# The merge stage's widening products as three float32r passes, with their weights in the split ring, the merge's entry and exit waits and the row stage's pacing changed

## The chip, the cores and the metric

One Trainium2 chip; the kernel runs on one NeuronCore. The metric is the device time of one launch in microseconds (us). Its engines are TensorE (PE in the profile; PEld is its weight loads), VectorE (DVE), ScalarE (ACT), GpSimd (POOL) and SyncE (SP), which issues the DMAs. Each has its own in-order instruction stream, and they meet at semaphores.

## The reference, cut to what matters

Three blocks are applied to x, a [1024 tokens, 1024 features] float32 matrix. The change lies in the last part of the first block:

```python
branches = jnp.stack([y_a, y_b, y_c], axis=0)               # three branches, 256 wide each
up = jnp.einsum('nbtw,nwd->nbtd', branches, w_up)           # widened to 1024: the "up" products
gates = jax.nn.sigmoid(jnp.stack([gate_logits_a, gate_logits_b, gate_logits_c], axis=0))
merged = jnp.sum(gates * up, axis=0)
out = jnp.einsum('btd,de->bte', merged, w_out)
return layer_norm(DEEPNORM_ALPHA * x + out, ln_g, ln_b)
```

The second block begins with an RMS norm of this result and a projection of it (its v columns are computed in the same stage as `out`).

## The kernel before, in words

Everything is float32. Large products are made from float32r operands: a value is split into a high half (ScalarE copies it as float32r) and a low half (VectorE subtracts the high half from it), and one product becomes three passes, high x high, low x high, high x low (`mm3`, L260, the passes at L263, L264 and L265).

Weights come in **units** of [128, 1024]. `Weights` (L287) keeps a ring of two raw units and of three split ones. SP loads unit i+1 when unit i-1 has been split (`w_load`, L313), ScalarE writes its high half (`w_hi_of`, L325, instruction at L332) once PE has finished the unit three before, VectorE the low half (`w_lo_of`, L340, instruction at L345). `early_units` lists all units in the order in which they are used; `OUT_W0`, `V_W0` and others are positions in that list. Each engine's program is a Python generator. `weave` advances several of them in turn, one `STEP` at a time, so the number of `STEP`s sets the order of instructions in an engine's stream.

Before the merge, gate tiles 0 to 15 (branches a and b) are computed as units, copied out and stored in DRAM. The merge then has eight steps, one for each d, a tile of 128 output features by 1024 tokens:

- PE (`merge_pe`, L933): one gate unit for branch c (`unit_pe`, 48 float32r passes of 512 columns), then `up_pe` for each of the three branches: 2 contraction tiles x 2 token halves, each one plain fp32 matmul (L928) of a 128x128 block of w_up with yT, the branch outputs transposed. So 12 such products per step. Banks of PSUM come from a ring of eight, `B.all`.
- ScalarE (`merge_act`): splits a weight unit, applies the sigmoid to two gate tiles read back (L1198), then to the gate unit's two halves (L1179).
- VectorE (`merge_dve`): splits a weight unit, then multiplies each product with its gate (L1521) and adds it to the merged tile (L1524), branch by branch.
- SP (`step_load`): reads back two gate tiles of 512 KB and loads three blocks of w_up of 128 KB into the tile `up` and one slot of h.

Ahead of the merge PE waits until the last early gate has been evicted (`sig_u`) and until VectorE has written the last part of yT (`ye`, L1501).

After the merge comes the **row stage**, `rows1_*`: 48 units, each used as the moving operand for groups of three, three and two token tiles (`GROUPS`). Units 0 to 23 of the stage are `out` (8 per group), units 24 to 47 are v (8 per group). A unit takes 18 passes for a group of three tiles and 12 for a group of two, L263 to L265. The merged tiles, as stationary operand, are split first: `m_hi` on ScalarE (L1241), `m_lo` on VectorE (L1589), tile 0 at the end of the merge, the others one per unit. When a group's 8 `out` units are done, VectorE adds x (L1607, "orow"), then come the layer norm's statistics (L1621), its root on ScalarE (L1272) and its two passes on VectorE (L1638, L1641); then the RMS norm of `norm_act`, `norm_dve` and `norm_pe`: squares (L437), scaling (L447), eight banks of PE transposes (L496), and the split of their results into `xs` (L457 on ScalarE, L482 on VectorE). PE has two banks for these transposes, so the third bank waits for the low half of the first. These programs are woven with the 48 units, two `STEP`s per unit. They begin at `OUT_AT` = 16, 32, 48 with different offsets on each engine.

Of the kernel before, what the change touches and what calls it, by code (L numbers as in the profile page):

```python
# [286 lines left out]
class Weights:  # L287
    def __init__(self, K, stack, units, first, depth=2, width=1024):
        self.units, self.first, self.start, self.depth, self.width = units, first, first, depth, width
        self.buf = K.sb(stack, "wring", [128, depth, width])  # L290
        self.parts = K.sb(stack, "wparts", [128, PARTS, 2, width], F32R)

    def raw(self, i):
        return self.buf[:, i % self.depth, :]

    def part(self, i, x):
        return self.parts[:, i % PARTS, x, :]
# [226 lines left out]
def b1_layout(K, A, st, h, xT, xs, W):  # L524
# [8 lines left out]
    up = K.sb(st, "up", [128, 4, 256])  # L533
# [23 lines left out]
    B.up = [[up[:, 0, :], up[:, 1, :]], [up[:, 2, :], up[:, 3, :]], [slots[2][:, 0:256], slots[2][:, 256:512]]]  # L557
# [10 lines left out]
    B.units, B.mm, B.all = Ring(K, K.banks[0:3]), Ring(K, K.banks[3:8]), Ring(K, K.banks)  # L568
# [67 lines left out]
def b1_sp(K, A, B):  # L636
# [13 lines left out]
    for i in range(2, ATT_W0 + 3):  # L650
        if i == 42:
# [3 lines left out]
            nc.sync.dma_start(B.h[:, 3:8, :], A["x"][:, 3:8, :]).then_inc(*sp.done("x_again", 0, by=16))  # L655
# [50 lines left out]
def up_load(K, A, B, j):  # L706
    br, d = divmod(j, 8)
    if d >= 2:
        K.sp.wait_ge(*(yield "up", j - 2, 1))
    K.nc.sync.dma_start(B.up[br][d % 2], A["wg"][j][:, 1024:1280]).then_inc(  # L710
        *K.sp.done("up_load", j, slot=f"{br}{d % 2}", by=16))


def step_load(K, A, B, d):
# [3 lines left out]
    for j in (d, 8 + d, 16 + d):  # L718
        yield from up_load(K, A, B, j)
# [197 lines left out]
def up_pe(K, B, j):  # L917
    nc, pe, br = K.nc, K.pe, j // 8
    pe.wait_ge(*(yield [("sb_y", 31), ("ye", 1, 0, 1), ("ye", 2, 1, 1)][br]))
    pe.wait_ge(*(yield "up_load", j))  # L920
    w = columns(B.up[br][j % 2])
# [4 lines left out]
    for k in range(2):  # L926
        for h, (b, _) in enumerate(banks):
            a = nc.tensor.matmul(b, w[:, k, :], B.yT[:, 2 * br + k, half(h)], start=(k == 0), stop=(k == 1))  # L928
            if k:
                a.then_inc(*pe.done("up", j, h))  # L930


def merge_pe(K, B):  # L933

    for d in range(8):
        yield from unit_pe(K, B.W, gate_unit(EARLY + d), B.xs, B.xkeys, B.all, "sig_u")
        for br in range(3):
            yield from up_pe(K, B, 8 * br + d)
# [3 lines left out]
def b1_pe(K, A, B):  # L942
# [9 lines left out]
    pe.wait_ge(*(yield "sig_u", gate_unit(EARLY - 1), 1))  # L952
    pe.wait_ge(*(yield "ye", 2, 1, 1))
# [4 lines left out]
    yield from weave(rows1_pe(K, B), *[later(OUT_AT[g] + 12, norm_pe(K, B, 2, g, B.turn)) for g in range(3)])  # L958
# [278 lines left out]
def m_hi(K, B, i):  # L1237
    K.act.wait_ge(*(yield "u", OUT_W0 - 1, 1))
# [28 lines left out]
def norm1_act(K, B, g):  # L1267
# [5 lines left out]
    yield STEP  # L1273
    yield STEP
# [318 lines left out]
def rows1_dve(K, B):  # L1593
    nc, dve = K.nc, K.dve
    for n in range(48):
        if n < 7:
            yield from m_lo(K, B, n + 1)
        if n == 8:
            for part in range(2):
                dve.wait_ge(*(yield "x_again", part))  # L1600
        if n in (8, 16, 24):
            for t in GROUPS[n // 8 - 1]:
# [11 lines left out]
def norm1_dve(K, B, g):  # L1614
# [20 lines left out]
    for t in ts:  # L1635
# [6 lines left out]
            *dve.done("ln_b", t))  # L1642
        yield STEP
# [2154 lines left out]
def build_program(nc, A):  # L3798
    with ExitStack() as ctx:
# [106 lines left out]
def host1(I):  # L3906
# [10 lines left out]
    A["wg"]=np.ascontiguousarray(np.concatenate([G,U],2))  # L3917
# [85 lines left out]
```

## Time and profile before

| | us |
|---|---|
| median of 3 runs | 2908.21 |
| lowest, highest | 2908.03, 2910.93 |
| profiled execution | 2909.24 |
| its span, first to last instruction | 2907.9 |

The mean granted TensorE clock of the profiled execution is 0.986 of full speed. In a timeline row the first number is the start in us from the span's start, the second the duration in us; in brackets stands the idle time of the engine before it and what ended it ("issue": nothing that the profile shows). `ps` is PSUM, `wparts` the split weights, `wring` the raw ones, `xs` the split left operand, `merged`, `xT`, `h` and `b1t` tiles in SBUF. PE's matmuls are pipelined, so a pass's duration is longer than the distance between the starts of two. In a window row the length of the window comes first, then for PE, PEld, DVE, ACT and POOL the busy us with the number of instructions, then the granted clock, the DMA share and GB/s.

### The profile page before, as it was taken

What the parts mean: (1) busy time and instruction counts of PE and PEld (TensorE: products, weight loads), DVE (VectorE), ACT (ScalarE), POOL (GpSimd) and SP (SyncE); (2) the same over time, 40 slices, a digit from 0 to 9 for tenths busy, and PEclk for the clock granted to TensorE, in tenths of its full rate; (3) what the DMA queues carried; (4) which work ended last, traced back from release to release, by engine and by line L of the source; (5) the groups of instructions that cost most, each with busy time, mean ns of one, the idle gap of its engine ahead of it and who ended that gap; (6) DMA issues with size and microseconds to landing.
All of it is one profiled execution on the core that took longest, in us unless ns stands there. A gap on an engine that the chain in (4) does not pass through costs nothing.

```text
span 2907.9 us, 52327 instructions
## 1 busy us (share of the span) xinstructions
PE 2781.6 (96%) x21208; PEld 2181.1 (75%) x21208; DVE 1663.6 (57%) x3141; ACT 1268.5 (44%) x2321; POOL 222.5 (8%) x281
## 2 busy tenths in 40 slices
PE   8999999999999899999999999999898889999998
PEld 6766777776667777777777777777888878778776
DVE  3555656663347625655555556766566664652566
ACT  4344534322224536655556544344444434642234
POOL 0000000000000001111111001455310000000000
PEclk9999999999999999999999999999999999999999
DMA  3010120124224561343332334355844364521114
GB/s 129 30 37 30 44 58 30 52 73 166 89 80 129 159 191 46 82 104 81 85 83 74 111 112 154 131 167 186 287 134 162 126 247 139 160 91 44 37 61 156
DMA packets 188368, 316.58 MB, mean 109 GB/s; under 512 B 78288, under 2 KB 119520, under 8 KB 186464
## 3 DMA queue, kind: packets, MB, share of 16 engines
q1 hardware_dynamic: 188128, 313.23, 33.9%
q8 instruction: 168, 2.75, 0.4%
q14 instruction: 72, 0.59, 0.1%
HBM read 239.19 MB, written 73.99 MB: 108 GB/s over the span
## 4 chain that ended last, share of the span: by engine, by line
PE 79%; DVE 13%; ACT 5%; issue 2%; DMA 1%; DVEq 0%; SPq 0%; ACTq 0%
PE ps L263 19%; PE ps L265 18%; PE ps L264 18%; PE ps L2699 5%; PE ps L928 3%; PE ps L2405 3%; PE ps L2431 2%; PE ps L2418 2%; DVE wparts L345 2%; PE ps L853 1%; ACT wparts L332 1%; PE ps L827 1%; PE ps L801 1%; DVE mk__55 L3063 1%; DVE h L1443 1%
## 5 line engine op out<-in xcount | busy, mean ns | idle before, releaser
L263 PE MATMUL ps<-xs,wparts 128*128 128x512 f32 (+1 forms) x1664 | 702.0, 422 | 12.5 <-DVE xs L1548 9.2
L265 PE MATMUL ps<-xs,wparts 128*128 128x512 f32 (+1 forms) x1664 | 655.1, 394 | 0.0
L264 PE MATMUL ps<-xs,wparts 128*128 128x512 f32 (+1 forms) x1664 | 654.0, 393 | 0.0
L345 DVE TENSOR_TENSOR wparts<-wring,wparts 128x1024 fp32r<-128x1024 f32 x248 | 306.8, 1237 | 295.5 <-ACT wparts L332 271.3
L263 PEld LDWEIGHTS ps<-xs,wparts 128*128 128x128 f32 (+1 forms) x1664 | 312.9, 188 | 135.2 <-issue 73.0
L332 ACT ACTIVATE wparts<-wring 128x1024 fp32r<-128x1024 f32 x248 | 262.9, 1060 | 262.8 <-PE ps L265 184.2
L265 PEld LDWEIGHTS ps<-xs,wparts 128*128 128x128 f32 (+1 forms) x1664 | 312.7, 188 | 72.2
L264 PEld LDWEIGHTS ps<-xs,wparts 128*128 128x128 f32 (+1 forms) x1664 | 313.6, 188 | 57.2 <-issue 3.6
L2509 ACT ACTIVATE Pm<-Pm,ml 128x128 f32<-128x128 f32 (+1 forms) x384 | 168.2, 440 | 112.3 <-DVE ml L2580 112.0
L2580 DVE CUSTOM_DVE_ANT_0 Pm<-ps,mask 128x128 f32<-128x128 f32 (+1 forms) x384 | 110.9, 348 | 177.1 <-PE ps L2405 177.1
L2353 POOL COPY perm<-qkg 128x1024 f32<-128x1024 f32 x32 | 63.5, 2021 | 1493.9 <-ACT qkg L381 1223.6
L263 PE MATMUL ps<-wparts,mixA 128*128 128x512 f32 x320 | 128.1, 400 | 3.5 <-ACT vn L3531 2.6
L265 PE MATMUL ps<-wparts,mixA 128*128 128x512 f32 x320 | 125.4, 392 | 0.0
L264 PE MATMUL ps<-wparts,mixA 128*128 128x512 f32 x320 | 125.4, 392 | 0.0
L2592 DVE COPY PT<-ps 128x384 f32<-128x384 f32 (+1 forms) x160 | 92.3, 618 | 50.3 <-PE ps L2418 50.1
L263 PE MATMUL ps<-wparts,xs 128*128 128x512 f32 x256 | 105.3, 411 | 10.7 <-DVE wparts L345 7.1
L1443 DVE COPY_PREDICATED h<-lm,ps 128x512 f32<-128x512 uint8 x112 | 82.8, 739 | 38.9 <-PE ps L853 29.6
L264 PE MATMUL ps<-wparts,xs 128*128 128x512 f32 x256 | 103.0, 402 | 0.0
L265 PE MATMUL ps<-wparts,xs 128*128 128x512 f32 x256 | 102.4, 400 | 0.0
L263 PE MATMUL ps<-mixA,wparts 128*128 128x512 f32 x256 | 100.9, 394 | 1.4 <-DVE wparts L345 1.4
L264 PE MATMUL ps<-mixA,wparts 128*128 128x512 f32 x256 | 99.6, 389 | 0.0
L265 PE MATMUL ps<-mixA,wparts 128*128 128x512 f32 x256 | 99.6, 389 | 0.0
(412 smaller groups left out, 4853.0 us busy)
## 6 DMA issues: line engine op xcount, KB each, us to landing
wring<-in_wo SPq DMA_DIRECT2D x96, 512.0 KB, 3.5
ops<-rw SPq DMA_DIRECT2D x32, 640.0 KB, 6.5
wring<-in_w SPq DMA_DIRECT2D x39, 512.0 KB, 3.6
wring<-in_w2a SPq DMA_DIRECT2D x29, 512.0 KB, 6.0
wring<-in_w2u SPq DMA_DIRECT2D x28, 512.0 KB, 4.2
wring<-in_wg SPq DMA_DIRECT2D x24, 512.0 KB, 3.9
wring<-in_w2v SPq DMA_DIRECT2D x24, 512.0 KB, 4.0
MB<-wst SPq DMA_DIRECT2D x48, 256.0 KB, 5.0
```

Of the source, the lines that this page charges most:

```text
L263: nc.tensor.matmul(out, a, c, start=start, stop=False)
L264: nc.tensor.matmul(out, b, c, start=False, stop=False)
L265: return nc.tensor.matmul(out, a, d, start=False, stop=stop)
L332: K.nc.scalar.activation(W.part(i, 0), W.raw(i), ACT.Copy).then_inc(*K.act.done("w_hi", W.first + i))
L345: K.nc.vector.tensor_tensor(W.part(i, 1), W.raw(i), W.part(i, 0).bitcast(F32), ALU.subtract).then_inc(*K.dve.done("w_lo", W.first + i))
L928: a = nc.tensor.matmul(b, w[:, k, :], B.yT[:, 2 * br + k, half(h)], start=(k == 0), stop=(k == 1))
L1443: a = nc.vector.copy_predicated(dst, B.lmask[:, lev, :].unsqueeze(1).to_broadcast([128, 4, 128]), src)
L2405: a = nc.tensor.matmul(bank[:, lo:hi], qk[0][rr, half(c, 128)], qk[1][rr, 128 * (c - 1) if two else 128 * c:128 * c + 128], start=True, st ...
L2509: a = nc.scalar.activation(P, P, ACT.Exp, scale=-1.0, bias=ml[:, s.pi, c, h, 0:1], accum_out=ml[:, s.pi, c, h, 1:2])
L2580: a = nc.vector.tensor_tensor_reduce(B.Pm[:, (NS * p + i) % 3, h, lo:hi], K.bank["a_s", p, i, h][:, lo:hi], m, 1.0, 3e38, ALU.add, ALU.min ...
L2592: nc.vector.tensor_copy(B.PT[:, (NS * p + n) % 2, h, 0:w], K.bank["a_t", p, n, h][:, 0:w]).then_inc(*dve.done("a_pt", p, n, h))
L2699: a = nc.tensor.matmul(out[rr], lhs[rr], rhs[rr], start=start, stop=stop, skip_group_check=True)
```

## The change

- **The products.** `up_pe` makes each of the 12 products of a step from three float32r passes. The w_up blocks of a step become a unit of their own, 768 columns wide, in the same ring and list of units, behind the step's gate unit, so the stage has 16 units for 8 steps, and all later positions shift by 8. yT is split into `y_hi` and `y_lo`, six tiles of 1024 columns each, by ScalarE and VectorE at the start of the merge; `y_hi` lies where h[:, 2:8] is, `y_lo` where yT is.
- **The loads.** SP loads one such unit (384 KB) per step in place of the three blocks. The reload of x into h moves from the start of the merge (5 tiles) and its end (3 tiles) to three loads, one per group, at the end.
- **The entry.** PE's two waits ahead of the merge are gone. `B.all` is put together from the two rings that were in use, with what each bank waits for. ScalarE waits for `ye` instead.
- **The exit.** `m_hi` of tiles 0 and 1 follows the last gate unit; `m_lo` of tiles 0 and 1 stands between the branches of the last step on VectorE.
- **The row stage.** The RMS norm of each group begins five `STEP`s later on PE, ScalarE and VectorE.

```diff
-OUT_W0, V_W0, ATT_W0, PREP_W0, LATE_W0 = 47, 71, 95, 124, 152
+OUT_W0, V_W0, ATT_W0, PREP_W0, LATE_W0 = 55, 79, 103, 132, 160
...
 def gate_unit(j):
-    return B1[f"gate{j}"] if j < 7 else 23 + j
+    return B1[f"gate{j}"] if j < 7 else 23 + j if j < EARLY else 23 + 2 * j - EARLY
+def up_unit(d):
+    return gate_unit(EARLY + d) + 1
...
@@ early_units
+    merges = [w for d in range(8) for w in (A["wg"][EARLY + d], A["wu"][d])]
...
@@ b1_sp
-            nc.sync.dma_start(B.h[:, 3:8, :], A["x"][:, 3:8, :]).then_inc(*sp.done("x_again", 0, by=16))
...
-        if 42 <= i < 48:
-            yield from step_load(K, A, B, i - 40)
-        if i == 48:
+        if i in range(44, 56, 2):
+            yield from step_load(K, A, B, i // 2 - 20)
+        if i in (56, 58, 60):
+            g = i // 2 - 28
+            ts = slice(GROUPS[g][0], GROUPS[g][-1] + 1)
             sp.wait_ge(*(yield "merge", 15, 1))
             sp.wait_ge(*(yield "up", 23, 1))
-            nc.sync.dma_start(B.h[:, 0:3, :], A["x"][:, 0:3, :]).then_inc(*sp.done("x_again", 1, by=16))
+            nc.sync.dma_start(B.h[:, ts, :], A["x"][:, ts, :]).then_inc(*sp.done("x_again", g, slot=g, by=16))
...
-def up_pe(K, B, j):
-    nc, pe, br = K.nc, K.pe, j // 8
-    pe.wait_ge(*(yield [("sb_y", 31), ("ye", 1, 0, 1), ("ye", 2, 1, 1)][br]))
-    pe.wait_ge(*(yield "up_load", j))
-    w = columns(B.up[br][j % 2])
+def up_pe(K, B, d, br):
+    nc, pe, j, n = K.nc, K.pe, 8 * br + d, up_unit(d)
+    pe.wait_ge(*(yield "w_lo", n))
+    wh, wl = [B.W.part(n, x).rearrange("p (b k c) -> p b k c", b=3, c=128)[:, br] for x in range(2)]
...
     for k in range(2):
+        c = 2 * br + k
+        pe.wait_ge(*(yield "y_lo", c))
         for h, (b, _) in enumerate(banks):
-            a = nc.tensor.matmul(b, w[:, k, :], B.yT[:, 2 * br + k, half(h)], start=(k == 0), stop=(k == 1))
+            a = mm3(nc, b, (wh[:, k, :], wl[:, k, :]), (B.ys[0][:, c, half(h)], B.ys[1][:, c, half(h)]), k == 0, k == 1)
...
@@ b1_pe
-    pe.wait_ge(*(yield "sig_u", gate_unit(EARLY - 1), 1))
-    pe.wait_ge(*(yield "ye", 2, 1, 1))
+    u, m = B.units.n, B.mm.n
+    B.all = B.units.part([(u + x) % 3 for x in range(3)]).join(B.mm.part([(m + x) % 5 for x in range(5)]))
...
-    yield from weave(rows1_pe(K, B), *[later(OUT_AT[g] + 12, norm_pe(K, B, 2, g, B.turn)) for g in range(3)])
+    yield from weave(rows1_pe(K, B), *[later(OUT_AT[g] + 17, norm_pe(K, B, 2, g, B.turn)) for g in range(3)])
...
+def y_hi(K, B, c):
+    K.act.in_order()
+    K.nc.scalar.activation(B.ys[0][:, c, :], B.yT[:, c, :], ACT.Copy).then_inc(*K.act.done("y_hi", c))
+def y_lo(K, B, c):
+    K.dve.wait_ge(*(yield "y_hi", c))
+    K.dve.in_order()
+    K.nc.vector.tensor_tensor(B.ys[1][:, c, :], B.yT[:, c, :], B.ys[0][:, c, :].bitcast(F32), ALU.subtract).then_inc(
+        *K.dve.done("y_lo", c))
 def merge_act(K, B):
+    for c in range(6):
+        y_hi(K, B, c)
     for j in range(EARLY, 24):
         yield from gate_act(K, B, j, B.E, [("merge", j - 1, h) for h in range(2)] if j > EARLY else [],
                             more=in_turn(back_act(K, B, j - 16), back_act(K, B, j - 8)))
+        yield from w_hi(K, B.W, gate_unit(j) + 2)
...
@@ b1_act
+    act.wait_ge(*(yield "ye", 2, 1, 1))
     yield from weave(merge_act(K, B))
-    yield from m_hi(K, B, 0)
+    for i in range(2):
+        yield from m_hi(K, B, i)
...
@@ norm1_act, after the root
-    yield STEP
-    yield STEP
+    for _ in range(7):
+        yield STEP
...
@@ merge_dve
     for d in range(8):
         j = EARLY + d
         yield from w_lo(K, B.W, gate_unit(j) + 1)
-        for _ in range(7):
-            yield STEP
+        for c in range(0 if d else 6):
+            yield from y_lo(K, B, c)
         for br in range(2):
             yield from branch_dve(K, B, 8 * br + d, B.back[br][d % 2], [("sig", 8 * br + d)] * 2)
+            if br == 0:
+                yield from w_lo(K, B.W, gate_unit(j) + 2)
+            if d == 7:
+                yield from m_lo(K, B, br)
         yield from branch_dve(K, B, j, B.E, [("sig", j, h) for h in range(2)])
         yield STEP
-    yield from m_lo(K, B, 0)
...
@@ norm1_dve, after the layer norm
+    for _ in range(5):
+        yield STEP
     yield from norm_dve(K, B, 2, g, 10 - 3 * len(ts))
```

In `rows1_act` and `rows1_dve` the loop takes tile n + 2 (was n + 1), and VectorE waits for a group's own reload of x. The last diff part is shown as it acts: five more `STEP`s ahead of `norm_dve`.

## Rows read from the trace of the kernel before

**Rows 1.** The page, engines' share of the span, and the chain of waits by line

```profile
PE 2781.6 (96%) x21208; PEld 2181.1 (75%) x21208; DVE 1663.6 (57%) x3141; ACT 1268.5 (44%) x2321; POOL 222.5 (8%) x281
...
PE ps L263 19%; PE ps L265 18%; PE ps L264 18%; PE ps L2699 5%; PE ps L928 3%; PE ps L2405 3%; PE ps L2431 2%; PE ps L2418 2%; DVE wparts L345 2%; PE ps L853 1%; ACT wparts L332 1%; PE ps L827 1%; PE ps L801 1%; DVE mk__55 L3063 1%; DVE h L1443 1%
```

**Rows 2.** Windows of the merge steps: us, busy (instructions) per engine, PE clock, DMA share, GB/s

```profile
678.94:701.38 22.44, 22.44 (x71) 14.62 (x72) 5.60 (x8) 6.49 (x7) 0.00 (x0) 0.92 0.95 360
...
701.38:722.59 21.21, 21.21 (x74) 13.57 (x72) 8.15 (x12) 4.37 (x5) 0.00 (x0) 1.00 0.29 97
```

**Rows 3.** PE's lines by form (busy, mean ns), the widening products of the whole span

```profile
L928 PE MATMUL ps<-yT,up 128*128 128x512 f32 x128 | 56.2, 592 | 0.0
...
L928 PE MATMUL ps<-yT,h 128*128 128x512 f32 x64 | 28.8, 592 | 0.0
```

**Rows 4.** PE's timeline in the first merge step: start us, duration us

```profile
684.03 0.39 PE L263 MATMUL ps<-xs,wparts 128*128 128x512 f32 x1
...
690.83 0.39 PE L263 MATMUL ps<-xs,wparts 128*128 128x512 f32 x1
...
691.51 7.03 PE L928 MATMUL ps<-yT,up 128*128 128x512 f32 x16
```

**Rows 5.** The timeline where the merge starts (releaser of the idle time in brackets)

```profile
674.77 1.97 PE L905 MATMUL ps<-cc,h 128*128 128x128 f32 x16 [1.25 <-DVE h L1493]
...
675.52 3.32 DVE L1501 SCALAR_TENSOR_TENSOR yT<-ps,cols,yT 128x512 f32<-128x512 f32 x4 [0.81 <-PE ps L905]
...
678.94 0.47 PE L263 MATMUL ps<-xs,wparts 128*128 128x512 f32 x1 [2.20 <-issue]
...
680.69 0.63 PE L263 MATMUL ps<-xs,wparts 128*128 128x512 f32 x1
...
681.97 0.63 PE L263 MATMUL ps<-xs,wparts 128*128 128x512 f32 x1
```

**Rows 6.** The page, part 5: the two halves of a weight split

```profile
L332 ACT ACTIVATE wparts<-wring 128x1024 fp32r<-128x1024 f32 x248 | 262.9, 1060 | 262.8 <-PE ps L265 184.2
...
L345 DVE TENSOR_TENSOR wparts<-wring,wparts 128x1024 fp32r<-128x1024 f32 x248 | 306.8, 1237 | 295.5 <-ACT wparts L332 271.3
```

**Rows 7.** The timeline where the merge ends

```profile
846.83 3.60 PE L928 MATMUL ps<-yT,h 128*128 128x512 f32 x8
...
852.67 2.56 DVE L1589 TENSOR_TENSOR xs<-merged,xs 128x1024 fp32r<-128x1024 f32 x2
...
854.00 0.65 PE L263 MATMUL ps<-wparts,xs 128*128 128x512 f32 x1 [3.58 <-issue]
```

**Rows 8.** DMA issues from 849 to 880 us: KB each, median us to landing

```profile
h<-in_x SPq DMA_DIRECT2D x1, 1536.0 KB, 6.1
```

**Rows 9.** Windows of the row stage (the 48 units after the merge)

```profile
854.00:888.20 34.20, 34.20 (x144) 28.15 (x145) 19.52 (x17) 12.74 (x12) 0.00 (x0) 0.95 0.46 146
...
888.20:926.60 38.40, 36.61 (x160) 29.58 (x159) 28.07 (x36) 19.19 (x23) 0.00 (x0) 0.96 0.43 131
...
926.60:968.10 41.50, 30.37 (x120) 22.88 (x119) 31.13 (x41) 20.78 (x29) 0.00 (x0) 0.86 0.44 134
...
968.10:988.30 20.20, 18.97 (x86) 15.54 (x86) 18.37 (x26) 8.76 (x13) 0.00 (x0) 0.95 0.47 153
...
988.30:1064.60 76.30, 74.05 (x329) 59.63 (x328) 28.56 (x30) 33.85 (x44) 0.00 (x0) 1.00 0.58 177
```

**Rows 10.** The timeline in the row stage

```profile
910.74 0.50 PE L263 MATMUL ps<-wparts,xs 128*128 128x512 f32 x1 [1.79 <-DVE wparts L345]
...
925.38 4.66 DVE L1607 SCALAR_TENSOR_TENSOR h<-h,ps 128x512 f32<-128x512 f32 x6
...
932.16 0.55 PE L496 MATMUL ps<-cc,merged 128*128 128x128 f32 x3 [2.69 <-DVE xs L482]
...
952.93 0.66 PE L263 MATMUL ps<-wparts,xs 128*128 128x512 f32 x1 [3.56 <-DVE wparts L345]
...
966.88 1.62 PE L496 MATMUL ps<-cc,merged 128*128 128x128 f32 x6 [2.57 <-DVE xs L482]
```

More of the change, by code:

```diff
@@ L287, with columns @@
 class Weights:
+    def columns(self, i):
+        return slice(0, self.units[i].shape[1])
     def __init__(self, K, stack, units, first, depth=2, width=1024):
@@ L293, in raw @@
     def raw(self, i):
-        return self.buf[:, i % self.depth, :]
+        return self.buf[:, i % self.depth, self.columns(i)]
     def part(self, i, x):
-        return self.parts[:, i % PARTS, x, :]
+        return self.parts[:, i % PARTS, x, self.columns(i)]
 class Stretch:
@@ L567, in b1_layout @@
              Rec(4, 32, a[0], a[1], a[2], cells(B.vg), 4, B.cg, B.bd32, B1["cv1"], B1["cg1"], B1["ck"])]
-    B.units, B.mm, B.all = Ring(K, K.banks[0:3]), Ring(K, K.banks[3:8]), Ring(K, K.banks)
+    B.units, B.mm = Ring(K, K.banks[0:3]), Ring(K, K.banks[3:8])
     B.sb_s, B.sb_o = Ring(K, K.banks[3:6]), Ring(K, K.banks[6:8])
@@ L578, in early_units @@
 def early_units(A):
-    gates = lambda a, b: [A["wg"][j][:, 0:1024] for j in range(a, b)]
+    gates = lambda a, b: [A["wg"][j] for j in range(a, b)]
+    merges = [w for d in range(8) for w in (A["wg"][EARLY + d], A["wu"][d])]
     return ([A["w1"][i] for i in range(8)] + gates(0, 2) + [A["w1"][i] for i in range(8, 12)] + gates(2, 4)
-            + [A["w1"][i] for i in range(12, 16)] + gates(4, 7) + [A["w1"][i] for i in (22, *range(16, 22))] + gates(7, 24)
+            + [A["w1"][i] for i in range(12, 16)] + gates(4, 7) + [A["w1"][i] for i in (22, *range(16, 22))] + gates(7, EARLY) + merges
             + [A["wo1"][k] for _ in GROUPS for k in range(8)] + [A["w2v"][k] for _ in GROUPS for k in range(8)]
@@ L717, in step_load @@
         yield from gate_back(K, A, B, j)
-    for j in (d, 8 + d, 16 + d):
-        yield from up_load(K, A, B, j)
 def vrows_pe(K, B, i, ring):
@@ L926, in up_pe @@
     for k in range(2):
+        c = 2 * br + k
+        pe.wait_ge(*(yield "y_lo", c))
         for h, (b, _) in enumerate(banks):
-            a = nc.tensor.matmul(b, w[:, k, :], B.yT[:, 2 * br + k, half(h)], start=(k == 0), stop=(k == 1))
+            a = mm3(nc, b, (wh[:, k, :], wl[:, k, :]), (B.ys[0][:, c, half(h)], B.ys[1][:, c, half(h)]), k == 0, k == 1)
             if k:
-                a.then_inc(*pe.done("up", j, h))
+                a.then_inc(*pe.done("up", j, h, also=[("u", n, 1)] if br == 2 and h else []))
 def merge_pe(K, B):
@@ L937, in merge_pe @@
         for br in range(3):
-            yield from up_pe(K, B, 8 * br + d)
+            yield from up_pe(K, B, d, br)
         yield STEP
@@ L1245, in rows1_act @@
     for n in range(48):
-        if n < 7:
-            yield from m_hi(K, B, n + 1)
+        if n < 6:
+            yield from m_hi(K, B, n + 2)
         if n in (32, 40):
@@ L1595, in rows1_dve @@
     for n in range(48):
[L1596 to L1600, printed above, removed]
+        if n < 6:
+            yield from m_lo(K, B, n + 2)
         if n in (8, 16, 24):
+            dve.wait_ge(*(yield "x_again", n // 8 - 1))
             for t in GROUPS[n // 8 - 1]:
@@ L3810, in build_program @@
                 with ExitStack() as s2:
+                    K.sb(s2, "h_01", [128, 2, 1024])
+                    ys = [K.sb(s2, "y_hi", [128, 6, 1024], F32R)]
+                    K.sb(s2, "xT_and_cols", [128, 8216])
+                    ys += [K.sb(s2, "y_lo", [128, 6, 1024], F32R)]
+                with ExitStack() as s2:
                     h, xT = K.sb(s2, "h", [128, 8, 1024]), K.sb(s2, "xT", [128, 8, 1024])
                     b1 = b1_layout(K, A, s2, h, xT, xs, W)
+                    b1.ys = ys
                 with ExitStack() as s2:
```

21 lines of the change are left out of this document (6 added, 15 removed).

## The prediction

> **What bounds the kernel now.** I read the page first. TensorE is busy for 96% of the span, VectorE for 57%, ScalarE for 44%, and of the chain that ended last the fp32 widening products (L928) are 3% [rows 1]. So only what takes time out of PE's stream counts, and only where no other engine becomes late. The windows by merge step come next: seven of the eight steps take 21.21 us, with PE busy in all of it, the clock at 1.00, VectorE busy 8.15 us and ScalarE 4.37 us [rows 2]. The merge is PE's alone, and the other two have 13 and 17 us of room per step. The first step takes 22.44 us at a clock of 0.92 [rows 2]. Between the merge and the next stage there is a hole [rows 7]. The 48 row units that follow (out-projection, then v) are the only part near the change where PE is not alone: windows and timeline show PE held there by VectorE [rows 9, 10].
>
> **Part 1, the products.** A step holds 12 widening products. Each is two records of L928, so there are 192 records in all [rows 3]. Sixteen of them take 7.03 us, the last one 0.59 us long, so they start (7.03 - 0.59)/15 = 0.429 us apart, and one fp32 product costs 0.859 us [rows 3, 4]. A float32r pass of the gate unit next to it: from 684.03 to 690.83 us there are ten triplets, 6.80/30 = 0.2267 us a pass [rows 4]. Three passes cost 0.680 us, and a product becomes 0.179 us shorter. Check of the step before: 48 x 0.2267 + 24 x 0.429 = 21.18 us against 21.21 us measured. After: 84 x 0.2267 = 19.04 us. That is 2.16 us per step, 15.1 us over steps 2 to 8. The new shape (128 weights, 512 moving columns, operands split in SBUF) is the gate unit's own, so I take its pace.
>
> A float32r pass is slower in the trace than half of an fp32 product's record would say (0.2267 against 0.429/2 = 0.2145 us). The Trainium skill ("FP8 and Floating Point Precision", section "TensorE Precision Notes") says that true FP32 is four passes, and its "TensorE: Matmul & The Clock Gate" (section "Wait — 56ns, not 53.3ns?") gives N/2.4 GHz + 2.5 ns, 216 ns for N = 512, for a full-speed pass. By these one pass of four would go, 96 x 0.216 = 20.7 us in the whole merge instead of the rows' 96 x 0.179 = 17.2 us. I go by the rows.
>
> **Part 2, the splitting this needs.** Per step the ring now carries a second unit of 768 columns. Its halves cost about three quarters of 1.060 us on ScalarE and of 1.237 us on VectorE [rows 6], so 0.80 and 0.93 us. ScalarE goes to 5.2 us per step and VectorE to 9.1 us, of 19.04 us. Both are hidden behind PE: the halves of the next step's up unit are written while this step's products run, some 14 us ahead. If that cover were gone, 1.7 us a step would show, 14 us in all. SP no longer issues three small loads per step but one of 384 KB. Its queue waits for the split of two units earlier, a step ahead; the gate tiles it reads back are queued behind that and are needed a step later. I cost this at nothing.
>
> **Part 3, the start of the merge.** PE ends its transposes at 674.77 + 1.97 = 676.74 us and then idles 2.20 us, until VectorE has written yT at 675.52 + 3.32 = 678.84 us [rows 5]. The two waits ahead of the merge are dropped, and the first gate unit takes banks long free, so it starts at 676.74 us. It also misses most of the low clock: from 680.69 to 681.97 us three passes take 1.28 us, 0.427 us each, 0.200 us more than at full clock [rows 5]; eight passes ran so, 1.6 us. The gate unit's 48 passes would end at 687.6 us. The products now need y split: ScalarE starts at 678.84 us, writes six y_hi and one weight half (7 x 1.06 = 7.4 us, with gaps until 686.5 us); VectorE first splits that weight (687.7 us) and then y_lo(0), ready at 689.0 us. **PE waits 1.4 us.** After that one y_lo comes every 1.28 us [two in 2.56 us, rows 7] and PE uses one in 1.36 us, so no more wait. The products end at 689.0 + 8.2 = 697.2 us, against 701.38 us before [rows 2]: 4.2 us gained. Whether the clock falls at the start hardly matters, as this path is VectorE's; if the 1.4 us wait lowers it, 1.6 us come back.
>
> **Part 4, the end of the merge.** The last step ends at 701.38 + 7 x 21.205 = 849.8 us. The row stage starts at 854.00 us, since VectorE splits the first merged tile (m_lo) only at 852.67 us, after all of the last branch, and again eight passes run at half clock [rows 7]: 4.2 + 1.6 = 5.8 us. Now m_hi(0), m_hi(1) follow the last gate unit at once, with the eight products (8.2 us) as cover. VectorE's order, counted from the start of those products: two gated halves until 4.2, weight split 5.5, m_lo(0) 6.8, four halves of the second branch 9.7, m_lo(1) 11.0, third branch 13.9, m_lo(2) 15.1, split of row unit 2 at 16.4 us. PE needs these at 8.2 (m_lo(0)), 12.2 (m_lo(1)) and 16.3 us (m_lo(2), unit 2). All arrive, the last by a hair. The whole 5.8 us goes. The reload of x (1.5 MB, 6.1 us to landing [rows 8]) now comes in three pieces between the first row units' weights. The first delays unit 3's weights to about 15 us, needed at 20.4 us. Nothing, or up to 1.5 us.
>
> Sum of the merge: 15.1 + 4.2 + 5.8 = **25.1 us**.
>
> **Part 5, the row stage.** The pacing moves each group's RMS norm (square, scale, transposes, x halves) five half-units later on all three engines; the layer norm ahead of it stays. What PE loses now: the windows hold 32.6, 33.8, 24.2, 17.5 and 72.5 us of passes (18 or 12 a unit at 0.2267 us, 0.3 us a transposed bank) and last 34.2, 38.4, 41.5, 20.2 and 76.3 us [rows 9]. Lost are 1.6 (counted in part 4), 4.6, 17.3, 2.7 and 3.8 us.
> - The first stop, 1.79 us until unit 13's weights are split [rows 10], hangs on VectorE's residual adds and layer norm, which do not move. It stays, with its 1.6 us of low clock.
> - VectorE then works without a stop from the adds of group 1 at 925.38 us to the weight split that frees PE at 952.93 us [rows 10], 27.5 us. The transposes of group 0 fall into it with four banks now (2.69 us of wait for the first [rows 10]). Afterwards six of the eight fall into it. I walked through the new order: with unit 8's start as zero, group 1's adds begin at 34.9 (37.2 before), PE meets waits of 4.7, 1.9, 3.0 and 1.6 us at the third to sixth bank, and the weight split that PE waited 3.56 us for is there in time. Unit 24 starts at about 74 us, not 80.0.
> - For group 2 the same happens on a smaller scale: now 2.57 us [rows 10] before unit 24, then about 5 us of waits and 1.6 us of low clock after it, with all eight banks to come. Unit 28 starts at 99.3 instead of 100.1 us.
> - Group 2's own transposes move off ScalarE's first v evictions: a few tenths.
>
> I take -1 us. The walk has sums of twenty steps in it, so its bounds are wide: if the waits vanish, 10 us more (of the 24.6 us lost before unit 28); if they add up the other way, 10 us less.
>
> **Sum.** 25.1 + 1.0 = 26 us. The profiled execution took 2909.24 us (span 2907.9), 1.0 us above the median of 2908.21. 2909.24 - 26 = 2883.2, so 2882 to 2883 at the median's level; I say 2882.5.
>
> **Rivals.**
> - **The row stage gains too.** For it: 24.6 us are lost there now, and any shift can unlock them. Against: VectorE's work does not shrink. 26 + 10 = 36 us, about 2873.
> - **The row stage gives back.** Six transposed banks instead of four meet VectorE's busy stretch, each stop bringing low clock. 26 - 12: about 2894.
> - **The merge is held by splits.** The up unit's half, or the x reload ahead of the weights in SP's queue, comes late in each step. Rows 2 and 6 speak against it. At 1.7 us a step, 14 us: about 2897.
> - **The passes run at half a record's pace** (0.2145 us), as if without a gap: 96 x (0.859 - 0.644) = 20.7 us instead of 17.2, so about 2879. This is also what the skill's two sections above give. The gate unit's own 0.2267 us speaks against it.
> - **Slower.** Place: the transposes T2 to T7 of groups 0 and 1, each now waiting for a low half that stands in VectorE's queue behind adds, statistics and layer norm of the next group. If PE stood still through all of both stretches (27.5 us, and two thirds of it, 18 us, for the two-tile group), with the 3.4 us at unit 13 and 3 us of low clock, it would lose 52 us where it lost 24.6, against 25.1 gained: 2911. It decides when the loss there passes 49.7 us. PE's independent units between the transposes speak against it.
> - **The change does not do what it says**: the product's pace or waits stay as they were, within 0.2%: 2908.
>
> **Chances.** Forecast 0.62, row stage gains 0.13, gives back 0.12, held by splits 0.05, half-record pace 0.03, slower 0.02, no effect 0.03. The forecast's own range is 2877 to 2888 (1.6 us of clock, 1.5 us of DMA, a few us of the walk). With the row stage's two sides the range is 2872 to 2892. A measurement of this kernel tells about 0.2%, 6 us, from no change: faster 0.95, same 0.03, slower 0.02.
>
> **What would show it.** Right: merge steps of 19.0 us with the clock at 1.00; PE's first gate unit starting right behind the transposes, then one wait of 1 to 2 us for VectorE's y_lo; no hole ahead of the first row unit; VectorE near 9 us a step. In the row stage: the stop at unit 13 still there, the 3.56 us wait for a weight split gone, waits of 2 to 5 us at transposes. Wrong: steps above 19.5 us, a pass pace other than 0.227 us, PE waiting for wparts inside the merge, or a sum of row-stage losses far from 29 us.

## The result and the profile after

The changed kernel takes **2882.47 us** (median of 4 runs, 2880.15 to 2888.27), the kernel before 2909.57 us on the same chips (4 runs). The ratio is 0.9901, 95% interval 0.9889 to 0.9913. The forecast was 2882.5 us. The profiled execution took 2883.6 us with a span of 2882.2 us, 25.7 us below that of before.

The profile page after the change, engines' shares and the chain by line (L261 to L263 are the three passes, L263 to L265 before), answers to [rows 1]:

```profile
PE 2761.7 (96%) x21304; PEld 2195.0 (76%) x21304; DVE 1679.0 (58%) x3155; ACT 1282.4 (44%) x2335; POOL 223.8 (8%) x281
...
PE ps L261 19%; PE ps L263 18%; PE ps L262 18%; PE ps L2716 5%; PE ps L2422 3%; PE ps L2448 2%; DVE wparts L346 2%; PE ps L2435 2%; PE ps L849 1%; ACT wparts L333 1%; PE ps L823 1%; PE ps L797 1%; DVE mk__58 L3080 1%; DVE h L1457 1%; DVE ST L3113 1%
```

The fp32 products have left the chain, and VectorE's share is one point up.

**The merge.** Windows of the second and third merge step, in the columns of [rows 2]:

```profile
696.86:716.10 19.24, 19.24 (x85) 15.76 (x84) 12.85 (x18) 5.23 (x6) 0.00 (x0) 1.00 0.38 123
716.10:735.34 19.24, 19.24 (x85) 15.76 (x84) 9.11 (x13) 5.23 (x6) 0.00 (x0) 1.00 0.30 103
```

A step takes 19.24 us instead of 21.21 us, still with PE busy in all of it. VectorE works 9.11 us (12.85 us in the second step, which ends what is left of y_lo and of the first step's products), ScalarE 5.23 us. The entry, against [rows 5]:

```profile
673.95 1.97 PE L901 MATMUL ps<-cc,h 128*128 128x128 f32 x16 [1.25 <-DVE h L1507]
...
675.67 0.48 PE L261 MATMUL ps<-xs,wparts 128*128 128x512 f32 x1
...
678.05 6.52 ACT L1200 ACTIVATE y_hi<-yT 128x1024 fp32r<-128x1024 f32 x6 [4.72 <-DVE yT L1515]
...
685.76 1.23 DVE L346 TENSOR_TENSOR wparts<-wring,wparts 128x1024 fp32r<-128x1024 f32 x1 [7.74 <-ACT wparts L333]
...
687.09 7.88 DVE L1206 TENSOR_TENSOR y_lo<-yT,y_hi 128x1024 fp32r<-128x1024 f32 x6
...
688.46 0.47 PE L261 MATMUL ps<-y_hi,wparts 128*128 128x512 f32 x1 [1.63 <-DVE y_lo L1206]
```

PE goes from the transposes into the gate unit without the 2.20 us gap and at full clock. Then it waits 1.63 us for y_lo: ScalarE writes six y_hi first, VectorE splits the second gate unit's weights (685.76 us) and only then y_lo. The exit, against [rows 7]:

```profile
828.42 1.23 DVE L1606 TENSOR_TENSOR xs<-merged,xs 128x1024 fp32r<-128x1024 f32 x1
...
831.54 0.39 PE L261 MATMUL ps<-wparts,xs 128*128 128x512 f32 x1
...
837.25 1.23 DVE L1606 TENSOR_TENSOR xs<-merged,xs 128x1024 fp32r<-128x1024 f32 x1
...
838.58 1.23 DVE L346 TENSOR_TENSOR wparts<-wring,wparts 128x1024 fp32r<-128x1024 f32 x1
...
839.86 0.19 PEld L261 LDWEIGHTS ps<-wparts,xs 128*128 128x128 f32 x1 [0.38 <-DVE wparts L346]
```

The first row pass (831.54 us) follows the last product without a gap; the first m_lo (L1606) was done two us earlier. The weight half of row unit 2 was done at 839.81 us, 16.6 us after the last step's products began, and PE's weight load waited 0.38 us for it, until 839.86 us; no pass shows a stop there.

**The row stage**, windows from unit 0, 8, 16, 24 and 28 on, against [rows 9] (there the last boundary is unit 28 too):

```profile
831.54:864.49 32.95, 32.95 (x145) 26.96 (x144) 23.55 (x23) 13.81 (x13) 0.00 (x0) 1.00 0.70 259
864.49:900.11 35.62, 33.20 (x146) 26.71 (x144) 26.32 (x34) 14.59 (x18) 0.00 (x0) 1.00 0.43 131
900.11:937.77 37.66, 30.02 (x120) 23.16 (x121) 29.66 (x38) 19.45 (x27) 0.00 (x0) 0.86 0.46 141
937.77:964.73 26.96, 21.75 (x94) 16.18 (x93) 20.68 (x27) 11.20 (x15) 0.00 (x0) 0.94 0.51 154
964.73:1038.40 73.67, 73.52 (x334) 60.19 (x332) 29.34 (x32) 37.40 (x49) 0.00 (x0) 1.00 0.59 176
```

PE's stops in it, against [rows 10]:

```profile
886.55 0.50 PE L261 MATMUL ps<-wparts,xs 128*128 128x512 f32 x1 [1.41 <-DVE wparts L346]
...
900.11 0.47 PE L261 MATMUL ps<-wparts,xs 128*128 128x512 f32 x1 [1.00 <-DVE h L1622]
...
912.34 0.90 PE L497 MATMUL ps<-cc,merged 128*128 128x128 f32 x3 [4.79 <-DVE xs L483]
...
920.67 0.55 PE L497 MATMUL ps<-cc,merged 128*128 128x128 f32 x3 [2.13 <-DVE xs L483]
...
940.26 0.50 PE L261 MATMUL ps<-wparts,xs 128*128 128x512 f32 x1 [0.96 <-DVE h L1622]
...
958.05 0.55 PE L497 MATMUL ps<-cc,merged 128*128 128x128 f32 x3 [2.81 <-DVE xs L483]
```

The stop at unit 13 is still there (1.41 us), the 3.56 us wait for a weight split is gone, and transposes wait 4.79, 2.13 and 2.81 us. Two stops of about 1 us are new: in units 16 and 24 PE now waits for VectorE's residual adds (L1622) to free its banks.

The last four of the 48 units, before and after: PE's stop ahead of unit 47, and ScalarE's half of that unit's weights, which waits for their DMA.

```profile
1059.23 1.06 ACT L332 ACTIVATE wparts<-wring 128x1024 fp32r<-128x1024 f32 x1 [3.73 <-DMA wring<-in_w2v]
1061.60 0.50 PE L263 MATMUL ps<-wparts,xs 128*128 128x512 f32 x1 [1.73 <-DVE wparts L345]
```

```profile
1033.11 1.06 ACT L333 ACTIVATE wparts<-wring 128x1024 fp32r<-128x1024 f32 x1 [2.85 <-DMA wring<-in_w2v]
1035.49 0.50 PE L261 MATMUL ps<-wparts,xs 128*128 128x512 f32 x1 [0.15 <-DVE wparts L346]
```

Where the 25.7 us of span lie, from first passes in the two traces:

| stretch | before | after | difference |
|---|---|---|---|
| start to the y transposes | 674.77 | 673.95 | -0.8 |
| transposes to row unit 0 (the merge) | 179.23 | 157.59 | **-21.6** |
| row unit 0 to 8 | 34.32 | 32.95 | -1.4 |
| row unit 8 to 28 | 100.04 | 100.24 | +0.2 |
| row unit 28 to the last pass | 75.91 | 73.42 | -2.5 |
| the rest | 1843.63 | 1844.05 | +0.4 |

### The profile page after: what moved, and what is told of

It is laid out like the page before. It is cut to its first block, busy times and chain, and to the rows that moved or that the text cites. A ratio compares the mean times of both kernels' runs of the same rounds, so it can differ in the third digit from the quotient of the medians.

```text
span 2882.2 us, 52558 instructions
## 1 busy us (share of the span) xinstructions
PE 2761.7 (96%) x21304; PEld 2195.0 (76%) x21304; DVE 1679.0 (58%) x3155; ACT 1282.4 (44%) x2335; POOL 223.8 (8%) x281
## 4 chain that ended last, share of the span: by engine, by line
PE 76%; DVE 15%; ACT 5%; issue 2%; DMA 2%; DVEq 0%; SPq 0%; ACTq 0%
PE ps L261 19%; PE ps L263 18%; PE ps L262 18%; PE ps L2716 5%; PE ps L2422 3%; PE ps L2448 2%; DVE wparts L346 2%; PE ps L2435 2%; PE ps L849 1%; ACT wparts L333 1%; PE ps L823 1%; PE ps L797 1%; DVE mk__58 L3080 1%; DVE h L1457 1%; DVE ST L3113 1%
## 5 line engine op out<-in xcount | busy, mean ns | idle before, releaser
L261 PE MATMUL ps<-xs,wparts 128*128 128x512 f32 (+1 forms) x1664 | 699.1, 420 | 10.6 <-DVE xs L1565 9.3
L263 PE MATMUL ps<-xs,wparts 128*128 128x512 f32 (+1 forms) x1664 | 654.1, 393 | 0.0
L346 DVE TENSOR_TENSOR wparts<-wring,wparts 128x1024 fp32r<-128x1024 f32 (+1 forms) x256 | 314.4, 1228 | 296.4 <-ACT wparts L333 271.2
L261 PEld LDWEIGHTS ps<-xs,wparts 128*128 128x128 f32 (+1 forms) x1664 | 312.6, 188 | 131.8 <-issue 69.0
L333 ACT ACTIVATE wparts<-wring 128x1024 fp32r<-128x1024 f32 (+1 forms) x256 | 269.7, 1054 | 311.5 <-PE ps L263 215.4
L263 PEld LDWEIGHTS ps<-xs,wparts 128*128 128x128 f32 (+1 forms) x1664 | 312.6, 188 | 72.2
L261 PE MATMUL ps<-wparts,mixA 128*128 128x512 f32 x320 | 128.7, 402 | 3.4 <-ACT vn L3548 2.6
L263 PE MATMUL ps<-wparts,mixA 128*128 128x512 f32 x320 | 125.7, 393 | 0.0
L261 PE MATMUL ps<-wparts,xs 128*128 128x512 f32 x256 | 104.5, 408 | 3.5 <-DVE h L1622 2.0
L263 PE MATMUL ps<-wparts,xs 128*128 128x512 f32 x256 | 102.2, 399 | 0.0
L261 PE MATMUL ps<-mixA,wparts 128*128 128x512 f32 x256 | 100.8, 394 | 0.5 <-DVE wparts L346 0.5
L263 PE MATMUL ps<-mixA,wparts 128*128 128x512 f32 x256 | 99.6, 389 | 0.0
```

Source lines behind the costliest of these rows:

```text
L261: nc.tensor.matmul(out, a, c, start=start, stop=False)
L263: return nc.tensor.matmul(out, a, d, start=False, stop=stop)
L333: K.nc.scalar.activation(W.part(i, 0), W.raw(i), ACT.Copy).then_inc(*K.act.done("w_hi", W.first + i))
L346: K.nc.vector.tensor_tensor(W.part(i, 1), W.raw(i), W.part(i, 0).bitcast(F32), ALU.subtract).then_inc(*K.dve.done("w_lo", W.first + i))
```

## The experiments

The merge's length is the same to 0.01 us in every profile that leaves its code alone, so these small effects are read from stretches of the trace. The medians move by 2 to 5 us from chip to chip and run to run: the kernel before had 2909.57, 2911.39, 2911.48 and 2914.69 us, the changed one 2882.47 and 2884.04 us.

**1. Pacing undone**, in the changed kernel:

```diff
-later(OUT_AT[g] + 17, norm_pe(...))
+later(OUT_AT[g] + 12, norm_pe(...))
...
-    for _ in range(7):        # norm1_act
+    for _ in range(2):
...
-    for _ in range(5):        # norm1_dve
-        yield STEP
```

> The changed kernel with the row stage's RMS norm put back five steps earlier on all three engines. My theory: the merge (entry, products, exit) makes the whole gain and the pacing is worth about nothing, so 2882.5 + 1 = 2883 us, row stage 207 to 208 us from the first pass of unit 0 to the last of unit 47 (206.6 after the change), with the 3.6 us wait for a weight split in group 1's stretch back again and the waits at transposes smaller. Rival: the pacing is worth several us by itself, then 2887 us or more. The other rival: it costs, then 2880 us or less.

Measured: 2886.67 us, ratio to before 0.9915 (0.9900 to 0.9930), whose interval overlaps the changed kernel's own. The median lies just under my rival's 2887 us, so it decides little. The profile says more: unit 8 to unit 28 takes 100.44 us (100.24 with the pacing). The whole row stage takes 208.9 us, more than the 207 to 208 us I gave. Of these 2.3 us over the changed kernel, 0.6 are in units 0 to 8, whose length the pacing by itself leaves alone (34.3 us in the kernel before and in run 2), 0.2 in units 8 to 28, and 1.6 behind unit 28, of which units 28 to 44 have 0.4. Who PE waited for from unit 8 to unit 28, in total us, times and longest:

```profile
PE ps L497 <- DVE xs L483: 10.3, 8, 2.7
PE ps L261 <- DVE wparts L346: 5.0, 2, 3.6
```

The weight-split waits are back (5.0 us), and the transposes wait 10.3 us in eight pieces instead of 10.8 us in six. Nearly the same time is lost in other places.

**2. Pacing alone**, in the kernel before (the same edit reversed).

> The kernel before with only the five steps of pacing. My theory: row stage, unit 8 to unit 28, stays at 100 us, so 2908 to 2910 us. Rival (the pacing carries part of the 27 us): 2900 to 2905 us. If it carries the opposite sign without the merge's changes: above 2912 us.

Measured: 2910.97 us, ratio 1.0004 (0.9994 to 1.0014). Unit 8 to 28 takes 100.60 us (100.04 without the pacing), units 28 to 44 take 62.3 us (62.7). The pacing moves waits and gains nothing that counts, with or without the rest.

**3. Exit undone**: m_hi and m_lo of the first tile after the merge, as before.

```diff
@@ b1_act
-    for i in range(2):
-        yield from m_hi(K, B, i)
+    yield from m_hi(K, B, 0)
@@ merge_dve
-            if d == 7:
-                yield from m_lo(K, B, br)
...
+    yield from m_lo(K, B, 0)
@@ rows1_act, rows1_dve: tile n + 1 again instead of n + 2
```

> The changed kernel with the first merged tiles split after the merge again, as before. My theory: a hole of 4 us with PE idle ahead of the first row unit, then eight passes at 1.2 GHz (1.6 us): 2882.5 + 5.8 = 2888 us. Rival: the hole is caught up in the row stage, where PE waits for VectorE anyway: then the hole shows but the waits before unit 28 shrink by as much, and the time stays below 2885 us.

Measured: 2890.77 us, ratio 0.9926 (0.9910 to 0.9943). PE's first row pass:

```profile
836.54 0.54 PE L261 MATMUL ps<-wparts,xs 128*128 128x512 f32 x1 [4.21 <-issue]
```

The merge is 161.96 - 157.59 = 4.4 us longer, and units 0 to 8 take 34.33 us instead of 32.95, 1.4 us more, with eight passes at the low clock (granted clock 0.54 from 836.54 to 839.80 us). Together 5.8 us, as expected. Units 24 to 28 took 25.4 us here instead of 27.0, but so they did in two kernels with the exit left alone (experiments 5 and 7), so that is not the hole being caught up.

**4. Entry waits back**:

```diff
-    u, m = B.units.n, B.mm.n
-    B.all = B.units.part(...).join(B.mm.part(...))
+    pe.wait_ge(*(yield "sig_u", gate_unit(EARLY - 1), 1))
+    pe.wait_ge(*(yield "ye", 2, 1, 1))
+    B.all = Ring(K, K.banks)
```

> The changed kernel with PE's two waits ahead of the merge and a fresh ring of banks. My theory: the gate unit starts 2.2 us after the transposes end, but the first product still waits for y_lo, so PE's wait there (1.6 us) goes and the step ends only 0.6 us later at full clock, 2.2 us later if the clock falls as it did before the change: 2883 to 2885 us. Rival: the entry is worth its full 2.2 us and 1.6 us of clock: 2886.5 us.

Measured: 2887.73 us, ratio 0.9920 (0.9905 to 0.9935). PE's first gate unit:

```profile
677.84 0.47 PE L261 MATMUL ps<-xs,wparts 128*128 128x512 f32 x1 [2.20 <-issue]
...
678.79 0.63 PE L261 MATMUL ps<-xs,wparts 128*128 128x512 f32 x1
...
680.07 0.63 PE L261 MATMUL ps<-xs,wparts 128*128 128x512 f32 x1
```

The 2.20 us gap is back and with it the low clock (three passes in 1.28 us), and PE does not wait for y_lo. The merge takes 159.74 us, 2.15 us more, as I expected for the case that the clock falls: the y_lo wait of the changed kernel takes back part of what the entry gives, so that the entry is worth 2.15 us, not 3.8. The median is above the 2883 to 2885 us I gave.

**5. fp32 products** in the changed kernel, on the high halves (the low halves are left out of the product but still computed):

```diff
-            a = mm3(nc, b, (wh[:, k, :], wl[:, k, :]), (B.ys[0][:, c, half(h)], B.ys[1][:, c, half(h)]), k == 0, k == 1)
+            a = nc.tensor.matmul(b, wh[:, k, :].bitcast(F32), B.ys[0][:, c, half(h)].bitcast(F32), start=(k == 0), stop=(k == 1))
```

> The changed kernel with each widening product as one plain fp32 matmul again, of the high halves alone (the low halves of weights and y are left out of the product; they are still computed). My theory: PE alone bounds the merge, so each step takes 48 x 0.2270 + 12 x 0.859 = 21.2 us instead of 19.24 us, 8 x 1.97 = 15.8 us more: 2898 us. Rival: part of the step is held by the splits or by bank releases, then the steps are longer than 21.3 us or the difference is under 12 us.

Measured: 2903.85 us, ratio 0.9980 (0.9968 to 0.9992), runs up to 2910.7. The window of the third step:

```profile
719.94:741.14 21.20, 21.20 (x75) 13.58 (x73) 9.11 (x13) 5.22 (x6) 0.00 (x0) 1.00 0.27 93
```

21.20 us, as before the change, with all the splitting of the change in it: VectorE 9.11 us, ScalarE 5.22 us, and PE never waits. The merge is 172.86 - 157.59 = **15.3 us** longer. That is what the passes alone are worth. The median is 21.4 us above the changed kernel's, 6 us more than that explains. The seven runs lie in two clusters, 2901.8 to 2903.9 and 2907.9 to 2910.7 us; in the profiled one, the lowest, the span is 18.3 us longer, and of the other 3.0 us 2.0 lie behind the row stage, 0.7 in it and 0.3 ahead of the merge. What makes the rest is not shown.

**6. Two passes** instead of three (high weights by low y left out):

```diff
-            a = mm3(...)
+            nc.tensor.matmul(b, wh[:, k, :], B.ys[0][:, c, half(h)], start=(k == 0), stop=False)
+            a = nc.tensor.matmul(b, wl[:, k, :], B.ys[0][:, c, half(h)], start=False, stop=(k == 1))
```

> The changed kernel with two passes per widening product (high weights by the low half of y left out). My theory: 96 passes at 0.231 us less, 22 us: 2860 us, steps of 16.5 us with PE busy throughout, VectorE 9.1 us a step. Rival: at that length VectorE or ScalarE ends last, steps stay above 17.5 us. If the 0.2311 us pace of the products comes from the alternating moving operands y_hi and y_lo, it falls to 0.2267 us here.

Measured: 2873.07 us, ratio 0.9879 (0.9861 to 0.9898). The window of the fourth step, and PE's stops in row units 0 to 8:

```profile
728.20:744.50 16.30, 16.30 (x74) 13.50 (x73) 9.09 (x13) 5.22 (x6) 0.00 (x0) 1.00 0.35 123
```

```profile
820.25 0.50 PE L261 MATMUL ps<-wparts,xs 128*128 128x512 f32 x1 [1.34 <-DVE wparts L346]
...
833.83 0.50 PE L261 MATMUL ps<-wparts,xs 128*128 128x512 f32 x1 [1.01 <-DVE wparts L346]
```

ScalarE's weight half ahead of the second of them, which is unit 5's:

```profile
831.45 1.06 ACT L333 ACTIVATE wparts<-wring 128x1024 fp32r<-128x1024 f32 x1 [5.10 <-DMA wring<-in_wo]
```

The steps are 16.32 us with PE busy in all of it, the last one 16.69 us, and the merge is 20.9 us shorter. But only 14 us of that are in the span and some 10 in the median. Units 0 to 8 take 36.90 us instead of 32.95. With 5.4 us of products in the last step instead of 8.3, VectorE's branch products and m_lo no longer fit under them: the split of row unit 2 ends 1.3 us late (the first stop). The second stop comes from the DMA: unit 5's weights are issued at 822.93 us, 2.3 us behind the second reload of x, and land at 831.43 us, after 8.5 us (5.9 us in the changed kernel, where the same load also follows that reload); ScalarE waited 5.10 us for them. Part 4 had the first of these covers "by a hair" and put the reload at nothing, or up to 1.5 us; in the changed kernel ScalarE waits for such a DMA too, up to 6.0 us, but PE does not. I had expected the whole 22 us and no wait.

**7. y_lo first**:

```diff
-        yield from w_lo(K, B.W, gate_unit(j) + 1)
         for c in range(0 if d else 6):
             yield from y_lo(K, B, c)
+        yield from w_lo(K, B.W, gate_unit(j) + 1)
```

> The changed kernel with VectorE's six y_lo ahead of the weight split of the second gate unit. My theory: y_lo(0) is ready some 2.4 us after yT, long before the gate unit ends, PE's 1.63 us wait goes and nothing takes its place, as that weight split is needed 10 us later: 1.6 us less, 2881 us. Rival: the next y_lo or the later weight split becomes the wait, 0 to 1 us gained.

Measured: 2884.18 us, ratio 0.9909 (0.9895 to 0.9924), no different from the changed kernel in the median. PE's only wait in the whole merge is now the one ahead of the transposes:

```profile
PE ps L901 <- DVE h L1507: 1.3, 1, 1.3
```

The merge takes 155.72 us, 1.87 us less. The gain is there in the trace and below what the runs can tell.

**8. Half outer**: the loops over h and k exchanged.

> The changed kernel with the loops over token half and contraction tile exchanged in the products, so that PE stays in a PSUM bank for six passes instead of three. If the pace of 0.2311 us instead of 0.2267 us comes from changing banks, it falls to 0.229 us or below, 1 us in all; if it comes from the operands (y in place of xs), it stays at 0.2311 us and the time stays at 2882.5 us. The y_lo wait grows by about 0.1 us at most.

Measured: 2886.22 us, ratio 0.9916 (0.9901 to 0.9930). A step's 36 product passes still start 0.2311 us apart (707.09 to 715.18 us, 35 distances). Changing banks is not the cause. PE waited for y_lo twice, 1.9 us in all, and the merge took 158.16 us, 0.6 us longer, where I had given 0.1 us.

**9. The same kernel again**, for the level of its chip.

> The changed kernel itself once more, as the level for the runs beside it. My theory: 0.990 to 0.991 of the kernel before, merge and row stage as in its first profile.

Measured: 2884.04 us, ratio 0.9894 (0.9878 to 0.9911); merge 157.59 us, unit 8 to 28 100.57 us.

**10. Splits on GpSimd**, with y_lo first, beside run 9:

```diff
+ON_POOL = [OUT_W0 + n for n in (12, 13, 18, 20, 22, 26, 28)]
...
+    for n in ON_POOL:        # b1_pool
+        K.pool.wait_ge(*(yield "w_hi", n))
+        K.pool.in_order()
+        K.nc.gpsimd.tensor_tensor(W.part(n, 1), W.raw(n), W.part(n, 0).bitcast(F32), ALU.subtract).then_inc(
+            *K.pool.done("w_lo_pool", n, also=[("w_lo", n)]))
```

> The changed kernel with y_lo first (1.6 us less) and with the low halves of row units 12, 13, 18, 20, 22, 26 and 28 written by GpSimd, which is idle in this stage. My theory: what is lost in the row stage between units 8 and 28 is VectorE's queue, so 7 x 1.24 = 8.7 us less work there brings 4 to 8 us, 2875 to 2879 us. Rival: GpSimd takes over 5 us for one split of 1024 columns, or slows VectorE beside it, and PE waits for GpSimd's halves instead: 2884 us or more.

Measured: 2881.05 us (2879.11 to 2882.68; run 9 gave 2883.16 to 2886.83), ratio 0.9885 (0.9870 to 0.9899). Of the 3 us, 1.9 are y_lo. The row stage took 206.7 us, 0.6 less than in run 9; units 8 to 28 took 99.06 us (100.57 in run 9, but 99.48 in run 7, which has y_lo first and nothing on GpSimd). GpSimd's first two splits, and what VectorE did beside them:

```profile
876.39 5.93 POOL L621 TENSOR_TENSOR wparts<-wring,wparts 128x1024 fp32r<-128x1024 f32 x2 [875.94 <-ACT wparts L333]
```

```profile
875.44 1.28 DVE L1660 SCALAR_TENSOR_TENSOR h<-h,st,xT 128x1024 f32<-128x1024 f32 x1
876.76 3.31 DVE L1663 SCALAR_TENSOR_TENSOR h<-h,st,xT 128x1024 f32<-128x1024 f32 x1
880.10 3.30 DVE L1660 SCALAR_TENSOR_TENSOR h<-h,st,xT 128x1024 f32<-128x1024 f32 x1
883.44 1.28 DVE L1663 SCALAR_TENSOR_TENSOR h<-h,st,xT 128x1024 f32<-128x1024 f32 x1
```

GpSimd needs 2.4 us for a split (2.38 to 3.18) where VectorE needs 1.23, and VectorE's layer norm pass, which reads two tiles in SBUF, takes 3.31 and 3.30 us beside it instead of 1.28. The Trainium skill ("SBUF — State Buffer", section "Who interferes with whom") says that a VectorE instruction with two SBUF inputs contends with a GpSimd instruction that reads SBUF. The trace agrees: the first of these passes starts 0.37 us after a GpSimd split of 2.6 us and takes 2.0 us more than usual. Not every split costs this. Four of the seven met such a pass and delayed it by 2.0, 2.0, 2.0 and 0.9 us. The other three met only VectorE instructions with one input in SBUF, and these took their usual time:

```profile
902.07 2.38 POOL L621 TENSOR_TENSOR wparts<-wring,wparts 128x1024 fp32r<-128x1024 f32 x1 [19.75 <-ACT wparts L333]
```

```profile
903.28 2.88 DVE L1643 BATCH_NORM_STATS2 st<-h 128x6 f32<-128x512 f32 x4
```

So VectorE was spared 7 x 1.23 = 8.6 us and lost 6.9 us. My theory (4 to 8 us) did not hold. Of the rival one half held, VectorE being slowed, and the other did not: PE waited for none of GpSimd's halves. It is the fastest version with all three passes that was measured; its gain over run 9 is mostly y_lo's.

**11. No y_lo read**: the third pass reads y_hi (low half of y left out, pass count kept). A single run, 2887.86 us.

> The changed kernel with the third pass of each widening product reading y_hi in place of y_lo (the low half of y is left out of the result, the number of passes stays). If the pace of 0.2311 us comes from the alternation between the two tiles as moving operand, it falls to 0.2267 us, steps of 19.05 us; if it comes from three passes per bank or from the 768-column weights, it stays at 0.2311 us and steps at 19.24 us.

The products of one step, in the changed kernel and in this one:

```profile
746.26 0.39 PE L261 MATMUL ps<-y_hi,wparts 128*128 128x512 f32 x1
...
753.89 0.39 PE L261 MATMUL ps<-y_hi,wparts 128*128 128x512 f32 x1
```

```profile
746.56 0.39 PE L261 MATMUL ps<-y_hi,wparts 128*128 128x512 f32 x1
...
754.04 0.39 PE L261 MATMUL ps<-y_hi,wparts 128*128 128x512 f32 x1
```

The rows are the first passes of the first and of the twelfth triplet. 33 distances in 7.63 us are 0.2312 us each, in 7.48 us 0.2267 us each. The steps took 19.04 us.

## Why the prediction was right, point by point

- **Part 1, the products** (15.1 us over seven steps, 17.2 us in all by the rows). Measured: 21.21 - 19.24 = 1.97 us a step, 13.8 us over seven. The term was mis-sized by 1.3 us: I took the gate unit's 0.2267 us, and passes that change to y_lo run at 0.2311 us, which is 0.16 of the 0.20 us a step. A pass pace other than 0.227 us was one of my own signs of being wrong, and it appeared; it was worth too little to move the forecast out of its range. Run 5 isolates the passes at 15.3 us, entry included. The half-record pace (20.6 us by its own terms, not the 20.7 written) did not happen; the rows' pace was too fast already. Nor did the 20.7 us that the Trainium skill's two sections gave: a pass took 0.2267 or 0.2311 us here, not 0.216.
- **Part 2, the splits at nothing.** Right: no step waits (run 5 has the steps at the old length with all splits in them). Run 6 shows how little of the cover is spare at the exit, while its steps stay PE's at 16.32 us. VectorE at 9.11 us and ScalarE at 5.23 us were the forecast values.
- **Part 3, the entry** (4.2 us). Right in each link: the start behind the transposes, no low clock, then the wait, 1.4 us forecast, 1.63 measured. From the start of the transposes to the second step it was 26.6 us before and 22.9 after, 3.7 us; of the missing 0.5 us the pace of the products is 0.16 and the longer wait 0.2. Run 4 values the dropped waits alone at 2.15 us, run 7 the y_lo wait at 1.9.
- **Part 4, the exit** (5.8 us). Right: run 3 gives 4.4 + 1.4 us. The order of VectorE's instructions held, each within 0.4 us: the last one came at 16.6 us for 16.4, which PE needed at 16.3.
- **Part 5, the row stage** (-1 us). The sign was a guess of the walk and is not borne out: +0.2 us between units 8 and 28, and runs 1 and 2 give -0.2 and +0.6 us for the pacing. Behind unit 28 the "few tenths" came: units 28 to 44 take 62.7 us without the pacing and 62.3 with it. The walk was close in detail (unit 24 at 74 us against 73.3, unit 28 at 99.3 against 100.2, first transpose wait 4.7 against 4.79 us) and missed two things: the waits at units 16 and 24 for the residual adds, and that the waits of 1.9, 3.0 and 1.6 us at the next three banks come out as none, 2.13 us and none; PE ran at half clock behind the first long wait (granted clock 0.50 from 912.3 to 916.0 us). VectorE worked without a stop in this stretch for 27.5 us before the change and for 26.8 us after it (899.27 to 926.03 us); that this sets the length either way fits the runs, but none took that work away.
- **The sum** of 26 us met 25.7 us of span and 27.1 us of medians partly by luck: the merge and exit gave 21.6 + 1.4 = 23.0 us where 25.1 were forecast, and 2.5 us came from units 28 to 47, where nothing was forecast but tenths. The pacing has 0.4 us of that. The other 2.1 us lie in the last four units: PE waits there for the weights of unit 47, 1.73 us before and 1.71 us in run 2, and 0.15 us after. Those weights landed 5.3 us after their issue before and 4.2 us after. Of this wait the other kernels with the change's merge show 0.2 to 1.1 us (0.59 in run 9), so a part of the 2.1 us is this one profile's. What makes the load faster is not shown; it was not tried by itself.
- **The rivals.** Row stage gains or gives back: neither (runs 1, 2). Merge held by splits: no; run 6 shows where that begins, at the exit. Slower by standing transposes: PE lost at most 4.79 us at one.

## What to carry to other kernels

Where one engine is busy through a whole stage and the others have half of it free, count that engine's instructions at their start-to-start distance, and each one saved comes through in full; read the distance from the very operands it will read. At the borders of the stage look for what the next stage waits for and can be computed under the last products: here two borders were worth some 8 us with no work saved. Moving a group of instructions past a stretch in which another engine has a full queue only moves the waits; what seems to count is that engine's queue. An idle engine can take work out of it only beside instructions that it does not slow: here GpSimd took 8.6 us over and cost 6.9 us, because four of its seven splits met a pass with two inputs in SBUF.

## What the hardware showed that was not expected

- Passes of the same shape start 0.2267 us apart as long as all read one SBUF tile as moving operand (xs, high and low halves; or y_hi alone, runs 6 and 11), and 0.2311 us apart when two passes read y_hi and the third y_lo, which lie in separate tiles, whatever the bank order (run 8), and with VectorE busy for 12.85 us of a step or for 9.11. Whether the distance of the tiles or something else in their addresses does it stays open; other placements were not tried.
- An idle time of 1.25 us followed by transposes and then by passes without a gap left the granted clock at full (the entry after); the same with a further 2.20 us of idle time dropped it to its lower level, 1.2 GHz, for eight passes (before, and run 4: granted clock 0.50 from 679.2 to 680.8 us).
- A VectorE pass with two SBUF inputs went from 1.28 to 3.3 us beside a GpSimd subtraction of 2.4 to 3.2 us; VectorE's statistics (one input, 0.7 us each) and its instructions with one input in PSUM and one in SBUF kept their times beside the same subtraction.
